# Convolution matmuls behind the transposes of each attention turn, and a merge stage with three modulation buffers

## The reference, cut to what matters

```
mod  = silu(c) @ w_ada + b_ada                      # 6 x 1024 modulation values; 4 x 1024 are needed late
h    = modulate(rmsnorm(x), sh1, sc1);  p = h @ w_in
o    = 8 heads of attention, 512 queries x 768 keys, softmax, @ values
y_conv = (b_gate * dwconv3(c_gate * x_in)) @ w_conv_out      # x_in, b_gate, c_gate are columns of p
y_attn = o @ w_attn_out
x    = x + g1 * ((sigmoid(p_attn) * y_attn + sigmoid(p_conv) * y_conv) @ w_o)
x    = x + g2 * conv_ffn(modulate(rmsnorm(x), sh2, sc2))     # w_up, w_down
out  = rmsnorm(x)
```

## Time and profile before

| | |
|---|---|
| median of 3 runs | 907.83 us (905.94 to 908.05) |
| profiled execution | 908.06 us, of which the span from the first to the last instruction is 906.3 us |
| PE busy | 834.3 us (92%) |
| DVE busy | 498.8 us (55%) |
| ACT busy | 377.0 us (42%) |
| POOL busy | 368.7 us (41%) |
| mean granted TensorE clock | 0.963 of full |

### The profile page before, as it was taken

How to read it: one execution, slowest core, us unless ns; L and a number is a source line. 1 busy time by engine, 2 the same in 40 slices (tenths; PEclk the granted TensorE clock), 3 DMA queues, 4 the chain that set the end, 5 groups by cost and what they waited for, 6 DMA issues and landing times.

```text
span 906.3 us, 11419 instructions
## 1 busy us (share of the span) xinstructions
PE 834.3 (92%) x3960; PEld 685.9 (76%) x3960; DVE 498.8 (55%) x604; ACT 377.0 (42%) x577; POOL 368.7 (41%) x187
## 2 busy tenths in 40 slices
PE   6679969888888799999989989999999999999995
PEld 4458757777777688888857888888888888888884
DVE  5862898776767637877631486655555555100014
ACT  7763445445444442322132445444444444221134
POOL 0193455232433255554453314544444444444420
PEclk9989989999999899999999989999999999999998
DMA  8822212010110138877544213333333332332202
GB/s 313 279 64 53 59 36 71 24 47 24 35 37 24 47 117 250 234 230 237 171 135 160 70 48 93 116 93 93 95 106 100 93 93 93 108 102 93 93 24 93
DMA packets 126238, 96.21 MB, mean 106 GB/s; under 512 B 13468, under 2 KB 111033, under 8 KB 126201
## 3 DMA queue, kind: packets, MB, share of 16 engines
q1 hardware_dynamic: 126169, 95.71, 34.9%
q10 hardware_dynamic: 32, 0.01, 0.0%
HBM read 93.60 MB, written 2.10 MB: 106 GB/s over the span
## 4 chain that ended last, share of the span: by engine, by line
PE 63%; issue 12%; DVE 10%; POOL 6%; DMA 3%; ACT 3%; SPq 1%; POOLq 0%; ACTq 0%; DVEq 0%
PE ps L367 17%; PE ps L369 17%; PE ps L368 17%; PE ps L1416 7%; POOL wlo L311 5%; DVE small L1013 2%; PE ps L1398 2%; PE ps L1387 2%; DMA raw<-w_in_dram 2%; DVE work L988 1%; DVE small L1011 1%; PE ps L1482 1%; POOL ht L511 1%; DVE work L992 1%; DMA xt<-x_dram 1%
## 5 line engine op out<-in xcount | busy, mean ns | idle before, releaser
L311 POOL TENSOR_TENSOR wlo<-raw,whi 128x1024 fp32r<-128x1024 f32 (+2 forms) x130 | 299.7, 2311 | 478.5 <-ACT whi L303 478.4
L367 PE MATMUL ps<-hhi,whi 128*128 128x512 f32 (+1 forms) x552 | 213.3, 386 | 9.0 <-DVE hlo L928 5.8
L368 PE MATMUL ps<-hlo,whi 128*128 128x512 f32 (+1 forms) x552 | 211.9, 384 | 0.0
L369 PE MATMUL ps<-hhi,wlo 128*128 128x512 f32 (+1 forms) x552 | 211.6, 383 | 0.0
L303 ACT ACTIVATE whi<-raw 128x1024 fp32r<-128x1024 f32 (+2 forms) x131 | 127.5, 982 | 129.5 <-PE ps L369 86.7
L367 PEld LDWEIGHTS ps<-hhi,whi 128*128 128x128 f32 x552 | 105.6, 191 | 30.2 <-issue 3.7
L369 PEld LDWEIGHTS ps<-hhi,wlo 128*128 128x128 f32 x552 | 105.6, 191 | 20.1
L368 PEld LDWEIGHTS ps<-hlo,whi 128*128 128x128 f32 x552 | 105.7, 191 | 19.9 <-issue 0.2
L1189 DVE SCALAR_TENSOR_TENSOR work<-ps,prm,work 128x511 f32<-128x511 f32 x44 | 33.0, 749 | 73.5 <-ACT work L851 72.6
L1083 DVE SCALAR_TENSOR_TENSOR adacc<-ada,cvec,adacc 128x1024 f32<-128x1024 f32 x28 | 64.9, 2336 | 14.2 <-DMA ada<-w_ada_dram 14.2
L367 PE MATMUL ps<-fhi,whi 128*128 (+1 forms) x176 | 69.2, 393 | 0.1
(11 more groups left out here) (235 smaller groups left out, 1477.9 us busy)
## 6 DMA issues: line engine op xcount, KB each, us to landing
raw<-w_up_dram SPq DMA_DIRECT2D x88, 256.0 KB, 3.1
raw<-w_in_dram SPq DMA_DIRECT2D x66, 256.0 KB, 3.4
ada<-w_ada_dram SPq DMA_DIRECT2D x32, 512.0 KB, 4.2
raw<-w_down_dram SPq DMA_DIRECT2D x44, 256.0 KB, 2.7
adaraw<-w_ada_dram SPq DMA_DIRECT2D x32, 256.0 KB, 4.9
raw<-w_o_dram SPq DMA_DIRECT2D x16, 256.0 KB, 3.2
xt<-x_dram SPq DMA_DIRECT2D x4, 512.0 KB, 6.4
raw<-w_attn_out_dram SPq DMA_DIRECT2D x8, 256.0 KB, 2.9
```

The lines of the kernel that those rows point to most:

```text
L311: ins = (engine or nc.gpsimd).tensor_tensor(out=l, in0=r, in1=h.bitcast(F32), op=ALU.subtract)
L367: pe.matmul(o, l[0], r[0], start=start, stop=False)
L368: pe.matmul(o, l[0], r[1], start=False, stop=False)
L369: return pe.matmul(o, l[1], r[0], start=False, stop=stop)
```

## The change

Two edits. In the attention stage `conv_piece(g)` moves from ahead of the O and T blocks to the end of PE's turn. In the merge stage `ada2` gets a third buffer (a gap behind it shrinks by as much), load n waits for addition n-3 and not n-2, and the additions are dealt out by a table, five for each of d = 0 to 3, four for d = 4 to 6 and none for d = 7. The hardware loops of the merge stage go, all eight tiles are written out on PE, ACT and DVE with the same instructions in the same order otherwise.

```diff
+ADA_ADDS = (5, 5, 5, 5, 4, 4, 4, 0)
-        ada2 = sb("ada2", [P, 2, D], scope=mrg)
-        sb("gap2", [P, 1536], scope=mrg)
+        ada2 = sb("ada2", [P, 3, D], scope=mrg)
+        sb("gap2", [P, 512], scope=mrg)
...
-                wait(sp, s("ada2_used"), n - 1)
...
-                sp.dma_start(ada2[:, g % 2, :], rows[:, (2 + g) * D:(3 + g) * D]).then_inc(s(f"ada2_loaded{g % 2}"), 16)
+                k, g = n // 4, n % 4
+                wait(sp, s("ada2_used"), n - 2)
+                sp.dma_start(ada2[:, n % 3, :], w_ada[k * P:(k + 1) * P, (2 + g) * D:(3 + g) * D]).then_inc(s(f"ada2_loaded{n % 3}"), 16)
...
             for d in range(DT):
-                for g in range(4):
-                    load_ada2(4 * d + g, d, g)
-                    if g < 3 and d + 1 < DT:
-                        gate_load(d + 1, g)
+                for m in range(max(3, ADA_ADDS[d])):
+                    if m < ADA_ADDS[d]:
+                        load_ada2(sum(ADA_ADDS[:d]) + m)
+                    if m < 3 and d + 1 < DT:
+                        gate_load(d + 1, m)
...
-            merge_lo(0, True)
-            with dve.Fori(1, 2) as i:
-                merge_lo(i, False)
+            for d in range(DT):
+                b, w = 4 * (d % 2), 3 * (d % 2)
+                for m in range(ADA_ADDS[d]):
+                    ada2_add(sum(ADA_ADDS[:d]) + m)
...
                 if g + 2 < HEADS * TT:
                     scores(g + 2)
-                conv_piece(g)
                 if t == 3:
                     output(h, 0, 0)
...
                 if t == 1 and h >= 1:
                     output(h - 1, 1, 1)
+                conv_piece(g)
```

More of the change, by code:

```diff
@@ L438, in _, with load_ada2 @@
                                   ukv[:, k, :, 0:NOPE]) for k in range(KVT)])
-            def load_ada2(n, k, g):
-                wait(sp, s("ada2_used"), n - 1)
-                if not isinstance(n, int):
-                    sp.sem_inc(s("load_turn"), 1)
-                rows = w_ada[k * P:(k + 1) * P, :] if isinstance(k, int) else w_ada[bass.ds(k * P, P), :]
-                sp.dma_start(ada2[:, g % 2, :], rows[:, (2 + g) * D:(3 + g) * D]).then_inc(s(f"ada2_loaded{g % 2}"), 16)
+            def load_ada2(n):
+                k, g = n // 4, n % 4
+                wait(sp, s("ada2_used"), n - 2)
+                sp.dma_start(ada2[:, n % 3, :], w_ada[k * P:(k + 1) * P, (2 + g) * D:(3 + g) * D]).then_inc(s(f"ada2_loaded{n % 3}"), 16)
             for j in range(CT):
@@ L772, in _ @@
             split_hi(act, U_MERGE + 3, 3)
[L774 to L795, removed]
+            for d in range(DT):
+                b, w = 4 * (d % 2), 3 * (d % 2)
+                for n in range(3):
+                    m = 3 * d + n
+                    if n < 2:
+                        used(act, U_MERGE + m)
+                        if d == 0:
+                            act.wait_ge(s("z_lo"), CT)
+                            act.wait_ge(s("o_lo"), HEADS)
+                        wait(act, s("m_lo"), d - 1)
+                        nc.scalar.activation(work[:, w + n, :], ps[:, b + n, :], ACT.Sigmoid).then_inc(s("g_sig"), 1)
+                    else:
+                        act.wait_ge(s("m_sum"), d + 1)
+                        nc.scalar.activation(mhi[:, d, :], work[:, w + 2, :], ACT.Copy).then_inc(s("m_hi"), 1)
+                    split_hi(act, U_MERGE + m + 4, m % SLOTS)
             split_hi(act, U_O + 4, 0)
@@ L1069, in _, with ada2_add @@
             output_value(HEADS - 1)
[L1071 to L1080, removed]
+            def ada2_add(n):
+                k, gg = n // 4, n % 4 * D
+                dve.wait_ge(s(f"ada2_loaded{n % 3}"), 16 * (n // 3 + 1))
+                if k == 0:
+                    nc.vector.tensor_scalar(adacc[:, gg:gg + D], ada2[:, n % 3, :], cvec[:, k, 0:1], None, ALU.mult).then_inc(s("ada2_used"), 1)
@@ L1081, in ada2_add @@
                 else:
                     dve.wait_ge(s("ada2_used"), n - 3)
-                    nc.vector.scalar_tensor_tensor(out=adacc[:, gg:gg + D], in0=ada2[:, g % 2, :], scalar=cv,
+                    nc.vector.scalar_tensor_tensor(out=adacc[:, gg:gg + D], in0=ada2[:, n % 3, :], scalar=cvec[:, k, 0:1],
                                                    in1=adacc[:, gg:gg + D], op0=ALU.mult, op1=ALU.add).then_inc(s("ada2_used"), 1)
[L1087 to L1105, removed]
@@ L1107, in _ @@
-            merge_lo(0, True)
-            with dve.Fori(1, 2) as i:
-                merge_lo(i, False)
+            for d in range(DT):
+                b, w = 4 * (d % 2), 3 * (d % 2)
+                for m in range(ADA_ADDS[d]):
+                    ada2_add(sum(ADA_ADDS[:d]) + m)
+                for n in range(2):
+                    used(dve, U_MERGE + 3 * d + 2)
+                    dve.wait_ge(s("g_sig"), 2 * d + n + 1)
+                    nc.vector.tensor_tensor(out=work[:, w + n, :], in0=ps[:, b + 2 + n, :], in1=work[:, w + n, :],
+                                            op=ALU.mult).then_inc(s("m_prod"), 1)
+                dve.wait_ge(s("m_prod"), 2 * d + 2)
+                wait(dve, s("m_lo"), d - 1)
+                nc.vector.tensor_tensor(out=work[:, w + 2, :], in0=work[:, w, :], in1=work[:, w + 1, :],
+                                        op=ALU.add).then_inc(s("m_sum"), 1)
+                dve.wait_ge(s("m_hi"), d + 1)
+                nc.vector.tensor_tensor(out=mlo[:, d, :], in0=work[:, w + 2, :], in1=mhi[:, d, :].bitcast(F32),
+                                        op=ALU.subtract).then_inc(s("m_lo"), 1)
@@ L1442, in _ @@
                 output(HEADS - 1, 1, part)
[L1445 to L1466, removed]
-                    for k in range(CT):
[L1468 to L1473, removed]
@@ L1475, in _ @@
-            merge(0, True)
-            with pe.Fori(1, 2) as i:
-                merge(i, False)
+            for d in range(DT):
+                b = 4 * (d % 2)
+                if d == 0:
+                    pe.wait_ge(s("p_exp"), HEADS * TT)
+                elif d == 1:
+                    pe.wait_ge(s("pt_lo"), HEADS * TT)
+                    pe.wait_ge(s("o_val"), HEADS)
+                    pe.wait_ge(s("c_z"), CT)
+                wait(pe, s("m_prod"), 2 * d - 2)
+                for n in range(2):
+                    m = 3 * d + n
+                    unit(U_MERGE + m)
+                    project(pe, ps[:, b + n, :], m % SLOTS, hhi, hlo).then_inc(w_used, 1)
+                m = 3 * d + 2
+                slot = m % SLOTS
+                unit(U_MERGE + m)
+                if d == 0:
+                    pe.wait_ge(s("z_lo"), CT)
+                    pe.wait_ge(s("o_lo"), HEADS)
+                for n in range(2):
+                    for k in range(CT):
+                        last = mm3(pe, ps[:, b + 2 + n, :], (tile_of(whi, slot, n * CT + k), tile_of(wlo, slot, n * CT + k)),
+                                   (qhi[:, 2 * k + n, :], qlo[:, 2 * k + n, :]), k == 0, k == CT - 1)
+                last.then_inc(w_used, 1)
```

## The result

The changed kernel takes 868.84 us (865.23 to 869.43, four runs) against 907.94 for the kernel before. The ratio is 0.9564, with a 95% interval of 0.9533 to 0.9595. The forecast was 870.

A forecast was written before the change was run, and what follows sets the result against it. PE, busy 92% of the span, bounds the kernel, so gains lie in its idle and slow time. Attention 35.3 plus merge 3.7 gives 39.0; 906.3 - 39.0 + 1.76 = 869.1, rounded up to 870 us, range 865 to 885.

The forecast's parts named there:

- The waits of the attention stage: Attention stage: 23.2 us of PE waits go; 0.7 us at T(0) and 1.1 us at C(30) come.
- The arrival at C(6): Attention, turn 6: PE reaches convolution piece C(6) 4.98 us after transposes T(5), when the product, needing 4.90, is there.
- The slow pace: Attention stage: matmuls at the low clock behind long PE waits return to full pace, saving 13.9 us.
- The stage as a whole: Attention stage: moving the convolution pieces saves 35.3 us net.
- The transposes' slack: Attention stage: ptlo ends 0.9 us before T(6), so transposes do not wait for DVE; cost taken as 0.
- The merge: End of merge stage: PE's waits for the last mlo and a w_o weight go, 3.7 us; the fifth addition costs 0.
- The limit of 9.5 us: Merge stage: PE notices DVE's products being late only from 9.5 us behind it.
- Transposes that wait for DVE: Rival, attention stage: transposes wait under weight splits, 9 to 18 us back, 879 to 888 us; chance 0.15.
- The slow pace stays: Rival, attention stage: low clock has another cause or the product chain slips; 13 to 14 us back, 883; chance 0.10.
- The merge becomes DVE's: Rival, merge stage: fifth additions delay POOL's splits and PE stops, 1 to 4 us, 871 to 874; chance 0.06.
- Slower than before: Rival, attention stage: DVE's round fits behind no PE turn, PE stops before all 32 transposes, 918 us; chance 0.02.
- The total: Whole kernel: 35.3 us from attention and 3.7 us from the merge, 39.0 us in all.

The follow-up runs named there:

- run with two pieces: Changed kernel with only the convolution pieces of g mod 8 = 0 or 6 behind the transposes, all others ahead as before; 885.26 us.
- The holds: Changed kernel with PE made to wait before the convolution piece in 8 of 32 turns, for DVE's subtraction (907.14 us) or ACT's first copy (877.27 us).
- even table: Changed kernel with four modulation additions in each of the eight merge tiles, still three buffers; 869.38 us.
- two buffers: Changed kernel with two modulation buffers instead of three, its table of additions kept; 869.01 us.
- six a tile: Changed kernel with the additions table 6,6,6,6,6,2,0,0; 871.01 us.
- third profile: Changed kernel unaltered, run once more beside the variant with C(0) back ahead of T(0); 868.57 us.
- first-piece run: Changed kernel with the very first convolution piece, C(0), put back ahead of the transposes T(0); 868.32 us.
- long holds: Changed kernel with PE waiting in 8 of 32 turns, between transposes and convolution piece, for DVE's subtraction of the same tile; 907.14 us.

## Why the prediction was right, point by point

**The waits of the attention stage.** Forecast: 23.2 us go, 0.7 and 1.1 come. In the first profile 0.56 (at T(27)) and 0.87 (at C(30)) came. T(0) waits 0.6 in the second; in the first and the third the low clock ahead of it makes PE late enough for it. The gate's, the copy's and the keys' waits are gone as worked out.

**The arrival at C(6).** 4.98 us after T(5) was forecast against a product at 4.90. T(6) starts 4.27 after T(5) and C(6) follows it at once, at 4.89. The sum by blocks was 0.1 us off, and the run with two pieces showed that both added blocks are needed.

**The slow pace.** Forecast 13.9 us. In the profile of before the pieces behind the eight long waits take 13.9 us more than at 2.4 GHz; after the change, none of this is left at those places and the clock there is 1.00. The holds show that waits bring it. The term has a counterpart that I did not see: a low clock at the head of the stage, in all three profiles of the changed kernel and absent in the one of before. Three variants with the same attention code and no low clock there (even table, two buffers, six a tile) have a stage of 150.8 us, the changed kernel 151.6 to 152.4, so it costs 0.8 to 1.6 us. The third profile shows that it can begin ahead of all that the move touches, and the first-piece run that it comes without a wait at T(0). Both profiles with the old order lack it, so that the move makes it more likely is not excluded.

**The stage as a whole.** 35.3 us forecast, 36.2 measured (35.4 and 35.6 in the other two profiles). Of this, waits give 23.2 - 1.4 = 21.8. The slow pace is more than the pieces alone: the granted clock, stretch by stretch, was short of full by 15.4 us in sum from 168 to 330 us before and by 1.7 us in the head after, so 13.7. The prediction left out the transposes and values at the low clock behind the pieces, above all behind C(30). The remaining 0.7 us no run separates.

**The transposes' slack.** Forecast 0.9 us at T(6): ptlo(5) ends at 171.50, 3.35 after T(5), and T(6) starts at 4.27, so 0.92. It held everywhere but once, at T(27), apart from the wait of T(0) for its normalisation.

**The merge.** Forecast 3.7 us, measured 5.05. The mechanism was right and the size was off: the waits of 1.1 and 2.65 us went, and with them about 1.1 us of slower matmuls behind the second, a cost that the prediction counts in the attention stage and leaves out here. The fifth addition was taken as free, and it was; the way there was wrong. I had the products up to 9.1 us late by d = 3, with 4.6 at d = 0. They were 2.5 late in each of the first four tiles, against 2.4 at d = 0 before; with two buffers and the same table d = 3 is 7.9 late, so it is the third buffer that keeps them there. The limit of 9.5 us agrees with the runs: no wait at 7.9 us late (two buffers), one of 0.57 after 9.6 (table of six).

**The rivals.** Transposes that wait for DVE: excluded by the waits, 0.6 to 1.2 us in all. The slow pace stays: excluded, the clock is 1.00 from 155 us on. The merge becomes DVE's: true with six or eight additions a tile, not with five. Slower than before: the long holds show what it takes, waits of 2.4 to 4.3 us in eight turns to lose all of the gain.

**The total.** 39.0 us forecast, 38.7 between the profiles: 36.2 + 5.05 + 0.4 in the rest (where `mod_rows` alone gave 0.7), less 2.95 in the head, which I read as the scatter of S(2)'s start. The medians differ by 39.1. So the stages gave 41.7 us, 2.7 more than forecast, and the head took as much back. That the sum met the result this closely is in part luck.

## What to carry to other kernels

When an instruction waits on a chain that starts at another block, count from that block: put what feeds the chain first and independent work between the feeder and the waiter, and check by the sum of block lengths that PE arrives no earlier than the chain. Price a long wait of PE at itself plus what may follow it at half clock: here all but two of the waits of 2.2 to 4.3 us in the attention stages of all profiles had slow pace behind them, in the profile of before 1.5 to 2.5 us each, and that was a third of the gain. When a queue holds two kinds of loads, look at what stands ahead of the next stage's first load: a third buffer or an earlier place gave nearly the same.

## What was not expected of the hardware

- In the long holds, waits of nearly the same length, 2.42 to 2.44 us, were followed by 2.4 GHz in two cases and by 1.2 GHz in one. Waits of some 0.6 and 0.9 us close together were followed by the low clock in one of three groups of the two-pieces kernel (the fourth group, 1.63 and 0.87, was too), and seven waits of 0.5 to 1.2 us standing alone were not in the one profile there is. The two waits of 1.5 us ahead of the attention loop were followed by it in some profiles and not in others.
- The DVE scaling of 128 values takes 0.16 us where POOL does nothing beside it, and under a POOL split it is stopped until the split ends, whichever part of it is left: 2.36 us before, 0.50 after. By the Trainium skill (SBUF — State Buffer, section Who interferes with whom) contention between DVE and GpSimd on the ports that they share is an exclusive lock, and the order of issue decides who blocks. The trace agrees: in both profiles the split started first, and the scaling ended with it (167.11 and 167.10 before, 169.84 and 169.83 after).
